# Down-projection weight loads moved from SyncE's queue to ScalarE's, in the expert stage of a hybrid MLA, GLA and MoE decoder layer

## What is computed

```python
logits = (xt @ w_router + b_router).astype(jnp.float32)
top_val, top_idx = lax.top_k(logits, TOP_K)
w_top = jax.nn.softmax(top_val, axis=-1)
...
for e in range(N_EXPERTS):
    a = xt @ w_gate_up[e] + b_gate_up[e]
    gate = jnp.minimum(a[:, :D_FF], SWIGLU_LIMIT)
    up = jnp.clip(a[:, D_FF:], -SWIGLU_LIMIT, SWIGLU_LIMIT)
    h = (up + 1.0) * gate * jax.nn.sigmoid(SWIGLU_ALPHA * gate)
    out = out + combine[:, e:e + 1] * (h @ w_down[e] + b_down[e])
```

## Time and profile before

| | |
|---|---|
| median of 3 runs | 1694.73 us (1693.62 to 1697.74) |
| the profiled execution: its own time, its span | 1693.71 us, 1691.9 us |
| busy in the span: TensorE, VectorE, ScalarE, GpSimd | 91%, 25%, 16%, 5% |
| share of the span in the chain that ended last: TensorE, DMA, VectorE | 73%, 16%, 7% |
| the loads of the expert stage | 128 of gate and up, 64 of down, 2048 KB each |

### The profile page before, as it was taken

The page is one execution under the profiler, slowest core; times in us unless marked ns, Lnnn a source line. Parts: engine busy times, 40 slices in busy tenths (PEclk is TensorE's granted clock), DMA queues, the critical chain, the costliest instruction groups (busy, mean ns, idle before and its releaser), DMA issues.

```text
span 1691.9 us, 18929 instructions
## 1 busy us (share of the span) xinstructions
PE 1534.5 (91%) x7698; PEld 845.0 (50%) x7698; DVE 431.3 (25%) x1044; ACT 262.7 (16%) x554; POOL 81.1 (5%) x104
## 2 busy tenths in 40 slices
PE   6987997799999978699999999999999999999985
PEld 4654775568888735533444344334434433443432
DVE  4234222421302263421222122122212211221214
ACT  1144223211111122101110111011101101110111
POOL 0044011010001100000000000000000000000000
PEclk9999998786999957699999999999999999999998
DMA  7256246141245613089999999999999999999971
GB/s 283 100 198 200 83 167 242 38 162 62 100 149 186 261 50 132 27 347 395 427 428 428 428 428 428 428 428 428 428 428 428 428 428 428 428 428 428 428 324 59
DMA packets 62293, 494.53 MB, mean 292 GB/s; under 512 B 5248, under 2 KB 6457, under 8 KB 37545
## 3 DMA queue, kind: packets, MB, share of 16 engines
q1 hardware_dynamic: 50760, 453.75, 64.9%
q0 software_dynamic: 11488, 40.15, 7.0%
HBM read 486.84 MB, written 7.05 MB: 292 GB/s over the span
## 4 chain that ended last, share of the span: by engine, by line
PE 73%; DMA 16%; DVE 7%; ACT 2%; issue 1%; SPq 0%; DVEq 0%; ACTq 0%
PE bank L1000 19%; PE bank L599 16%; DMA ring<-in_w_gate_up 15%; PE bank L1025 8%; PE bank L556 5%; PE bank L986 5%; PE bank L1037 4%; PE bank L569 3%; PE bank L989 2%; PE bank L1007 1%; PE bank L870 1%; PE bank L584 1%; PE bank L812 1%; PE bank L872 1%; DVE arena L1449 1%
## 5 line engine op out<-in xcount | busy, mean ns | idle before, releaser
L1000 PE MATMUL bank<-ring,arena 128*64 128x512 f32 x2048 | 457.2, 597 | 17.3 <-DMA ring<-in_w_gate_up 17.3
L1000 PEld LDWEIGHTS bank<-ring,arena 128*64 128x64 f32 x2048 | 140.5, 137 | 313.3 <-issue 266.2
L1025 PE MATMUL bank<-ring,arena 128*64 128x512 f32 x1024 | 230.0, 598 | 10.3 <-DMA ring<-in_w_down 10.3
L599 PE MATMUL bank<-normed,ring 128*128 128x264 f32 x752 | 184.2, 406 | 3.4 <-DVE normed L1468 3.4
L599 PEld LDWEIGHTS bank<-normed,ring 128*128 128x128 f32 x752 | 149.7, 201 | 33.8 <-issue 6.9
L1820 DVE TENSOR_TENSOR arena<-arena,bank 128x264 f32<-128x264 f32 x136 | 58.4, 429 | 383.0 <-PE bank L1037 381.5
L1025 PEld LDWEIGHTS bank<-ring,arena 128*64 128x64 f32 x1024 | 71.4, 137 | 151.9 <-issue 130.8
L1129 ACT ACTIVATE arena<-bank 128x264 f32<-128x264 f32 (+6 forms) x172 | 64.3, 378 | 314.1 <-PE bank L599 180.9
L1825 DVE TENSOR_SCALAR arena<-bank 128x512 f32<-128x512 f32 x32 | 22.0, 688 | 312.9 <-PE bank L1000 312.9
L986 PE MATMUL bank<-arena 128*128 128x128 f32 x544 | 82.4, 297 | 11.0 <-DVE arena L1820 8.4
L986 PEld LDWEIGHTS bank<-arena 128*128 128x128 f32 x544 | 69.1, 199 | 24.2 <-DVE arena L1820 14.0
(11 more groups left out here) (244 smaller groups left out, 1233.6 us busy)
## 6 DMA issues: line engine op xcount, KB each, us to landing
ring<-in_w_gate_up SPq DMA_DIRECT2D x128, 2048.0 KB, 21.9
ring<-in_w_down SPq DMA_DIRECT2D x64, 2048.0 KB, 19.5
ring<-in_w_in SPq DMA_DIRECT2D x10, 2048.0 KB, 9.8
out<-arena POOLq DMA_DIRECT2D x10, 512.0 KB, 5.3
arena<-in_state_gla POOLq DMA_DIRECT2D x8, 512.0 KB, 7.1
ring<-in_w_o_mla SPq DMA_DIRECT2D x2, 2048.0 KB, 8.3
ring<-in_w_o_gla SPq DMA_DIRECT2D x2, 2048.0 KB, 8.5
ring<-in_w_out SPq DMA_DIRECT2D x2, 2048.0 KB, 8.4
```

Source lines behind the costliest of these rows:

```text
L599: mm = nc.tensor.matmul(lin_bank(name)[0:m, 0:width], w(ring_name, nk, cols)[:, k, a:a + m], rhs[:, k, 0:width], start=(k == 0), stop=(k = ...
L1000: mm = nc.tensor.matmul(B[q // 2][CAP * (q % 2):CAP * (q % 2) + CAP, :], xg[:, k, CAP * e:CAP * e + CAP], slot(EXPERT_SLOT[j])[:, a:a + 51 ...
L1025: mm = nc.tensor.matmul(B[4][CAP * half:CAP * half + CAP, :], hT[:, c, CAP * (k // 4):CAP * (k // 4) + CAP], slot(EXPERT_SLOT[j])[:, a:a + ...
```

## The change

The down loads are taken out of SyncE's stream and issued by ScalarE in `down_out`, behind a wait for both down slots and ahead of the two copies. The first down load (expert 0) is still issued by SyncE before the stage. A new argument q tells `expert_pair` the experts to load, and `expert_rows` moves up so that both engines can use it.

```diff
-            def load_down(e, used):
-                dn = w_down[0, bass.ds(e, 1)].rearrange("o (h p c) n -> p (o h) c n", p=P, h=2)
-                for j in range(4, MOE_SLOTS):
-                    sp.wait_ge(S(f"slot{j}_used"), used)
-                    sp.dma_start(expert_rows(j), dn[:, j - 4]).then_inc(S(f"expert_slot{j}"), 16)
...
             load_gate_up(1, 1)
             with sp.Fori(1, NE - 1) as e:
                 load_gate_up(e + 1, e + 1)
-                load_down(e, e)
-            load_down(NE - 1, NE - 1)
...
-            def down_out(n, e):
+            def load_down(expert):
+                dn = w_down[0, bass.ds(expert, 1)].rearrange("o (h p c) n -> p (o h) c n", p=P, h=2)
+                for j in range(4, MOE_SLOTS):
+                    act.dma_start(expert_rows(j), dn[:, j - 4]).then_inc(S(f"expert_slot{j}"), 16)
+
+            def down_out(n, e, following=None):
+                act.wait_ge(S("slot4_used"), n + 1)
                 act.wait_ge(S("slot5_used"), n + 1)
+                if following is not None:
+                    load_down(following)
                 for half in range(2):
                     nc.scalar.copy(y_rows[CAP * e:CAP * e + CAP, 512 * half:512 * half + 512], B[4][CAP * half:CAP * half + CAP, :])\
                         .then_inc(S("y_rows"), 1)
 
-            def expert_pair(m, p, first):
+            def expert_pair(q, m, p, first):
                 n = 2 * m
                 if not first:
                     hidden_out(n - 1)
                 sigmoid(n)
                 if not first:
-                    down_out(n - 1, 1)
+                    down_out(n - 1, 1, 2 * q)
                 hidden_out(n)
                 sigmoid(n + 1)
                 gathered(m + p + 1)
                 act.wait_ge(S("weights_turned"), m + 1)
                 nc.scalar.copy(wselT, B[6][:, 0:T]).then_inc(S("weights_copied"), 1)
-                down_out(n, 0)
+                down_out(n, 0, 2 * q + 1)
```

More of the change, by code:

```diff
@@ L362, in hn_parts, with expert_rows @@
             return [(hn_tok[p0:p0 + n, tt, :].rearrange("t (k p) -> t k p", k=KC)[:, a:b, 64 * g:64 * g + 64], src[:, a:b, :]) for p0, a, b in parts]
+        def expert_rows(j):
+            return slot(EXPERT_SLOT[j]).rearrange("p (c n) -> p c n", n=2 * DFF if j < 4 else D)
         block = ctx.enter_context(nc.Block())
@@ L401, in _ @@
                     sp.dma_start(m_tok, mem_prompt[0].rearrange("(t p) d -> p t d", p=P)).then_inc(S("mem_loaded"), 16)
-            def expert_rows(j):
-                return slot(EXPERT_SLOT[j]).rearrange("p (c n) -> p c n", n=2 * DFF if j < 4 else D)
             def load_gate_up(e, used):
@@ L437, in _ @@
                     load_gate_up(0, p * NE)
-                    load_down(0, p * NE)
                     load_gate_up(1, p * NE + 1)
@@ L441, in _ @@
                         load_gate_up(e + 1, p * NE + e + 1)
-                        load_down(e, p * NE + e)
-                    load_down(NE - 1, p * NE + (NE - 1))
             turned(sp, "y4")
@@ L1403, in expert_pair @@
                 nc.scalar.copy(wselT, B[6][:, 0:T]).then_inc(S("weights_copied"), 1)
-                down_out(n, 0)
+                down_out(n, 0, 2 * q + 1)
             gathered(0)
-            expert_pair(0, 0, True)
+            expert_pair(0, 0, 0, True)
             with act.Fori(1, NE // 2) as q:
-                expert_pair(q, 0, False)
+                expert_pair(q, q, 0, False)
             hidden_out(NE - 1)
@@ L1415, in _ @@
                 with act.Fori(1, npass) as p:
+                    load_down(0)
                     gathered(p * (NE // 2 + 1))
-                    expert_pair(p * (NE // 2), p, True)
+                    expert_pair(0, p * (NE // 2), p, True)
                     with act.Fori(1, NE // 2) as q:
-                        expert_pair(p * (NE // 2) + q, p, False)
+                        expert_pair(q, p * (NE // 2) + q, p, False)
                     hidden_out(p * NE + (NE - 1))
```

## The result

The changed kernel takes 1716.04 us (1712.98 to 1717.84, 4 runs) against 1694.21 us (4 runs of before, one more than in the table above): ratio 1.0123, 95% interval 1.0102 to 1.0143, so 17 to 24 us slower. 1716.04 lies within the stated range of 1699 to 1723 and outside the forecast's own range of 1703 to 1714. The profiled execution took 1716.57 us, 22.9 above that of before.

What follows compares the result with a forecast made beforehand. The prediction took the DMA engines at 428 GB/s as the bound. Late issue at the start 3.4, loan 6.7 and late issue at the end 3.4 made 13.5 us on 1694.73, so 1708 us, range 1699 to 1723.

Steps and rivals of the forecast that it cites:

- The bound: Expert stage: the 16 DMA engines at 428 GB/s set the pace, 58.8 us a pair; TensorE's own work is hidden.
- Instructions, 0 us: 62 down loads move from SyncE to ScalarE, holding its copies back 0.7 us per `down_out`; cost 0, without cover 22 us.
- Late issue, 3.4 + 3.4 us: Slot 4's load is issued 3.44 us later, which costs +3.44 us at the stage's start and again at D(31).
- Halves between the queues: Where SyncE's and ScalarE's queues both have work, each gets half of the DMA engines; no bandwidth gained, loads interleave.
- the rival in which whole loads alternate: Queues take turns by whole loads, not packets: the loan term is 4.6, the time 1706 us; chance 0.12.
- The loan, 6.7 us: GU(31) slot 3 lands later, closer to D(30)'s last byte, paid once at the end: 6.7 us, bounds 0 and 9.5.
- The queue just does not run dry, and the mean stays at the 58.8 us of the bytes: Steady state of the expert pairs: the DMA engines always have loads left, so it costs nothing.
- The margin of 0.1 to 1.0 us: Rest of GU loads still queued when the next down load flows, going between 0.1 and 1.0 us from pair to pair.
- the dry engines: Rival: DMA engines run out of loads, +15 us for each us short in 15 pairs, 1723 us; chance 0.14.
- Its own signs of being wrong: Period of 59.5 us or more with DMA gaps, a rate other than 428, GU landings as before, TensorE waiting for copies.
- The waits that were to go: Each pair's two down waits and those for GU slots 0 and 1 vanish; TensorE waits 2 to 3 us for slot 3.

Runs made afterwards that it cites:

- one_queue_late: Kernel before, with SyncE waiting for both down slots and then issuing both down loads, no second queue: 1701.3 us, ratio 1.003.
- only_last_but_one_on_act: Kernel before, with ScalarE issuing only expert 30's two down loads, each when its slot is free: 1707.01 us, ratio 1.0057.
- the work behind slot 3: 14 identity transposes added behind the read of gate and up slot 3: changed kernel 1725.26 us, ratio 1.0185; kernel before 1694.13 us, ratio 0.9999.
- short filler: Changed kernel with 4 identity transposes, which compute nothing, ahead of the wait for gate and up slot 3: 1714.85 us, ratio 1.0116.
- scatter_ahead_of_slot3: Changed kernel with the last three scatter products moved ahead of the wait for gate and up slot 3: 1708.54 us, ratio 1.008.
- last_but_one_back_on_sp: Changed kernel with each down load issued when its slot is free and expert 30's put back on SyncE behind GU(31): 1706.87 us, ratio 1.0061.

## Why the prediction was right, and where it fell short

**The bound** was read rightly. 428 GB/s is the limit, and no run moved more over the stretch from 850 to 1600 us.

**Instructions, 0 us.** Right. ScalarE's two issues take 0.84 to 1.40 us, against the 0.7 of the prediction; no wait of TensorE in the steady state ends on a ScalarE copy, which would have been a sign of being wrong.

**Late issue, 3.4 + 3.4 us.** Right at the start: lateness 3.4 to the tenth in one_queue_late. At the end the changed kernel shows 4.2, of which 0.7 is because D(31) is read in 9.36 us where it took 4.99 + 3.65: TensorE waited 7.3 us first and read at the lower clock.

**Halves between the queues.** Right. DMA of the changed kernel from 1396 to 1404, with both queues at work:

```profile
DMA packets 225, 3.42 MB, mean 428 GB/s; under 512 B 16, under 2 KB 16, under 8 KB 16
...
q10 hardware_dynamic: 112, 1.84, 53.8%
q1 hardware_dynamic: 113, 1.59, 46.8%
```

112 packets and 113, at the full rate; 16 of them are under 512 B, and of the bytes 54% and 46% are the two queues' shares. This agrees with the round-robin between queues that have work, which the Trainium skill gives in "DMA: Bandwidth & Descriptors", section "Queues, rings and completion order". Whether turns are packets or whole loads the times can't tell, since both forecasts lie too close together, but the trace can. A packet of these loads is a row of 16 KB and takes an engine 0.61 us. The stretches 1398.85 to 1399.46 and 1399.46 to 1400.07, each 0.61 us long:

```profile
DMA packets 16, 0.26 MB, mean 430 GB/s; under 512 B 0, under 2 KB 0, under 8 KB 0
q1 hardware_dynamic: 15, 0.25, 94.7%
q10 hardware_dynamic: 1, 0.02, 6.3%
...
q10 hardware_dynamic: 15, 0.25, 94.5%
q1 hardware_dynamic: 1, 0.02, 6.3%
```

One packet on each of 16 engines from one queue, then one from the other. A turn is 0.61 us, not the 4.90 us of a load: the rival in which whole loads alternate falls.

**The loan, 6.7 us.** Right in kind, and near in size. The last pair shows it by its landings, worked out from each load's issue and time to landing and counted from the start of GU(0). Slot 3 of GU(31) lands 18.4 us later than before (at 1646.53, before at 1625.14), the last load of D(30) 12.2 us later (1650.19 and 1634.94). The order alone makes the difference, 6.1 us; less 0.3 to spare that is 5.8 against 6.7. In only_last_but_one_on_act D(30) is 9.8 us late, 9.5 forecast. Wrong in when it is paid: it is carried from the start.

**"The queue just does not run dry, and the mean stays at the 58.8 us of the bytes".** This step failed. The margin of 0.1 to 1.0 us was worked out with a read of 3.6 us for slot 3. In 6 of 15 pairs it took 5.1 to 5.4 us at the lower clock, which eats the margin, and the engines run dry, 9.6 us in the six dips. The last load of D(30) lands 12.2 us late where 3.4 was forecast, and these 8.8 us are the miss: D(30) starts 18.2 us late in place of 10.1, and that is most of what separates 1716 from 1708. The prediction had named the dry engines as a rival with 0.14 and priced it at 15 us for each us short, for other reasons (ScalarE's share, late issue, bandwidth) and in all 15 pairs. Its own signs of being wrong point there too: a rate other than 428 (here 424 from 850 to 1600 us, in the row below) and gaps in DMA, at a mean pair of 59.31 us just short of the 59.5 it named.

```profile
850.00:1600.00 750.00, 715.13 (x3574) 292.55 (x3570) 148.62 (x401) 76.42 (x137) 0.00 (x0) 0.99 1.00 424
```

So the range held the result because it took in about half of the dry case, not because the forecast's own account was complete. That the margin is that thin is shown by the work behind slot 3; that a long read at the lower clock is enough to use it up, by the pairs of equal wait in the short filler. What stays open is the share of the waits themselves: in the changed kernel every wait above 2.6 us has a long read behind it, so what such a wait alone would cost can't be read there.

**The waits that were to go.** Those for slots 0 and 1 of gate and up are gone. Of the waits for down loads one of 1.3 us is left in three of the pairs, and the waits for slot 3 are 0.7 to 3.2 us where 2 to 3 was forecast.

## What to carry to other kernels

One queue fed in the order of use is a priority: it lands first what is needed first. A second queue on the same saturated DMA engines brought no bandwidth here and let loads issued late overtake loads issued early; moving two loads cost 9.7 us. When the bytes are the bound, ask not only who issues a load but how early its slot comes back: giving the down slots back 7 us sooner gained 7.6 us, where no choice of queue tried here gained anything. And where a forecast rests on a margin of a microsecond, price what happens past it as a case of its own.

## What the runs showed of the hardware that was not expected

TensorE, busy almost without a break, read the next 16 matmuls at a granted clock of 0.50 after a wait of 2.67 us (5.35 us for 3.65), while after waits of 1.08 and 1.80 us they took 3.65. In the short filler waits of 2.07 us were followed by reads of 5.25 and 5.35 us, and once by one of 3.65; in scatter_ahead_of_slot3 waits of 2.83 and 2.90 us were followed by reads of 3.65, in last_but_one_back_on_sp waits of 3.26 and 3.27 us. So the length of one wait does not decide it alone.

With loads of 2 MB waiting in SyncE's queue and in ScalarE's, the 16 DMA engines took one packet of 16 KB from each queue in turn, 0.61 us a turn, and moved 428 GB/s together, as much as with one queue.
